# Strassen's scheme for the input projection of heads 1 to 3

## The reference: what is computed

```
xn = rmsnorm(x, norm_gain)
proj = jnp.einsum('btd,dp->btp', xn, w_in)
gb, gc, hc, zc, q, k, v, o, zm, ig, fg = jnp.split(proj, ...)
yc, conv_new = short_conv(gc * hc, conv_buf, conv_w)
y_conv = gb * yc * jax.nn.silu(zc)
...
```

## Time and profile before

| | |
|---|---|
| median of 3 runs | 1104.28 us (1104.0 to 1104.38) |
| span of the profiled execution | 1100.9 us; 3.4 us of the median lie outside it |
| TensorE busy | 1061.1 us (96%) |
| DVE, ACT, POOL busy | 540.9, 340.7, 257.9 us |
| moved by DMA | 108.74 MB, 99 GB/s in the mean |

### The profile page before, as it was taken

How to read it: one execution, slowest core, us unless ns; L and a number is a source line. 1 busy time by engine, 2 the same in 40 slices (tenths; PEclk the granted TensorE clock), 3 DMA queues, 4 the chain that set the end, 5 groups by cost and what they waited for, 6 DMA issues and landing times. The chain is left out here.

```text
span 1100.9 us, 17978 instructions
## 1 busy us (share of the span) xinstructions
PE 1061.1 (96%) x7180; PEld 602.0 (55%) x7180; DVE 540.9 (49%) x1008; ACT 340.7 (31%) x672; POOL 257.9 (23%) x333
## 2 busy tenths in 40 slices
PE   3999999999999999999999999999999999999995
PEld 3655546565666555656665556566655555444442
DVE  5786664556553434575534345655332323434333
ACT  6636434243402232434022324340213131111111
POOL 5012313021211323212113232121111121542422
PEclk9999999999999999999999999999999999999998
DMA  9484532033200322342003224310212062365651
GB/s 243 135 182 78 132 86 49 24 107 101 89 22 17 96 63 77 93 110 89 21 17 96 64 77 120 102 32 22 93 43 86 25 220 91 108 223 205 233 201 77
DMA packets 124184, 108.74 MB, mean 99 GB/s; under 512 B 42384, under 2 KB 109092, under 8 KB 124100
## 3 DMA queue, kind: packets, MB, share of 16 engines
q1 hardware_dynamic: 88192, 68.83, 22.0%
q0 software_dynamic: 7600, 25.03, 6.2%
q10 hardware_dynamic: 28308, 13.73, 4.8%
HBM read 65.43 MB, written 33.41 MB: 90 GB/s over the span
## 5 line engine op out<-in xcount | busy, mean ns | idle before, releaser
L800 PE MATMUL bank<-xTh,Wh 128*128 128x512 f16 (+2 forms) x1304 | 421.2, 342 | 5.7 <-DVE Wl L163 5.7
L801 PE MATMUL bank<-xTl,Wh 128*128 128x512 f16 (+2 forms) x1304 | 423.9, 342 | 0.0
L802 PE MATMUL bank<-xTh,Wl 128*128 128x512 f16 (+2 forms) x1304 | 423.6, 342 | 0.0
L802 PEld LDWEIGHTS bank<-xTh,Wl 128*128 128x128 f16 x1304 | 129.2, 99 | 120.3 <-issue 0.7
L800 PEld LDWEIGHTS bank<-xTh,Wh 128*128 128x128 f16 x1304 | 129.2, 99 | 113.4 <-DVE Wl L163 6.0
L801 PEld LDWEIGHTS bank<-xTl,Wh 128*128 128x128 f16 x1304 | 129.3, 99 | 108.8 <-issue 2.4
L809 PE MATMUL bank<-Wh,xTh 128*128 128x128 f16 x544 | 92.8, 219 | 0.6 <-DVE ysum L163 0.6
L811 PE MATMUL bank<-Wh,xTl 128*128 128x128 f16 x544 | 92.8, 219 | 0.0
L810 PE MATMUL bank<-Wl,xTh 128*128 128x128 f16 x544 | 92.8, 219 | 0.0
L163 ACT ACTIVATE tz<-bank 128x512 f32<-128x512 f32 x32 | 19.1, 598 | 148.4 <-PE bank L802 147.7
L672 POOL TENSOR_TENSOR ysumst<-ysum,ysumst 128x1024 f16<-128x1024 f32 x16 | 34.1, 2130 | 105.5 <-ACT ysumst L163 105.5
(11 more groups left out here) (336 smaller groups left out, 1520.5 us busy)
## 6 DMA issues: line engine op xcount, KB each, us to landing
wst<-in_w_in ACTq DMA_DIRECT2D x23, 512.0 KB, 3.9
xs<-in_x_prompt SPq DMA_DIRECT2D x22, 512.0 KB, 4.3
y_ops<-ysumst POOLq DMA_DIRECT2D x16, 512.0 KB, 3.2
w_ops<-xs SPq DMA_DIRECT2D x16, 448.0 KB, 4.5
wst<-in_w_in SPq DMA_DIRECT2D x13, 512.0 KB, 5.5
out<-xs POOLq DMA_DIRECT2D x11, 512.0 KB, 2.9
Wh<-y_ops SPq DMA_DIRECT2D x12, 448.0 KB, 3.6
Wl<-y_ops SPq DMA_DIRECT2D x12, 448.0 KB, 4.4
```

Source lines behind the costliest of these rows:

```text
L800: mm(out, wh[:, k, :], xh, start=(k == 0), stop=False)
L801: mm(out, wh[:, k, :], xl, start=False, stop=False)
L802: last = mm(out, wl[:, k, :], xh, start=False, stop=(k == KT - 1))
```

## The change

In heads 1 to 3 the eight tiles beside V are taken in four pairs, (K,Q), (GC,HC), (GB,ZC) and (O,ZM). For a pair, the two tiles of weights (each cut in two halves of the 1024) and the block of x (cut in two halves of 256 tokens and two of the 1024) are 2 x 2 matrices of parts. Seven products of 12 matmuls with 256 columns take the place of eight. Some of the products use sums of parts: three banks, XB, YB and QB, hold the results, and two of these are seeded with results formed before. ACT copies XB to YB after M1 (`y_seed`, needed by M6) and takes QB after M5 (`fifth`, tile p5s); DVE forms QB from p5s and YB after M6 (`q_seed`, needed by M7 and M3) and takes YB after M7 (`c22_read`, needed by M4). The order of the products is M1, M5, M6, M2, M7, M3, M4. The matmuls of the recurrence stand in between (`after_second`, `after_third`; a state chunk is a `stream_chunk`). The mixed tokens go by pairs too, with 24 + 36 matmuls of 80 columns, behind the pair or, for pairs 1 and 2, behind pair 1.

The parts of x and their sums (4.2 MB per block) are formed and written to DRAM in head 0: the sums by POOL (`token_sums`: one operation of 1024 and four of 256 for each of 16 units, within blocks 1 to 3), split by ACT and DVE (`S_TAKE` says behind which tile). SP streams them back in each block of heads 1 to 3.

For each head, DVE applies 9 gains to raw weights, POOL forms four sums of 512 columns per pair (`weight_sums`), and ACT and DVE split 17 tiles (`split_high`, `split_low`; `op_low` counts them, up to number 16). Part of it is done in block 3 of the head before (`prep`), the rest in block 0 (`late`). Many semaphores are merged, and some buffers and the places of w_out's operands are others.

The core of the diff:

```
+PAIRS = [(K, Q), (GC, HC), (GB, ZC), (O, ZM)]
+M1, M5, M6, M2, M7, M3, M4 = range(1, 8)
+A_11, A_12, A_21, A_22, X_S2, X_S3, X_S4, X_S1 = range(8)
...
+S_TAKE = [{}, {Q: 0, HC: 1, GB: 2, ZC: 3, O: 4, ZM: 5}, {Q: 6, HC: 7, GB: 8, ZC: 9, O: 10, ZM: 11}, {V: 12, HC: 13, O: 14, ZM: 15}]
+SPLITS = 17
+FIRST_SPLIT = [0, 5, 9, 13]
+V_SPLIT = 2
+T_SPLIT = [3, 7, 11, 15]
...
+            def load_operands(B):
+                b, at = B % NB, MIX + 4 * HALF * (B % 2)
+                sp.wait_ge(xa_out[b // 2], 16 * 8)
+                if B < NB:
+                    for i in range(2):
+                        sp.wait_ge(s_out[i], 32 * 2 * (b + 1))
+                for first, last in ((A_11, A_21), (A_22, X_S1 + 1)):
+                    for part in range(2):
+                        sp.dma_start(xT[part][:, first:last, at:at + 4 * HALF], x_ops[b, :, part, first:last, :]).then_inc(xo_in[B % 2], 16)
...
+            def weight_sums(g, p):
+                first, second = (raw_of(t) for t in PAIRS[p])
+                lo, hi = slice(0, KT // 2), slice(KT // 2, KT)
+                pool.wait_ge(op_low, splits(g, FIRST_SPLIT[p] + 1))
+                n = 16 * (g - 1) + 4 * p
+                for i, (out, x, y, op) in enumerate((
+                        (first[:, lo, :], second[:, lo, :], first[:, lo, :], ALU.subtract),
+                        (second[:, lo, :], second[:, hi, :], second[:, lo, :], ALU.subtract),
+                        (second[:, hi, :], first[:, lo, :], second[:, hi, :], ALU.subtract),
+                        (first[:, hi, :], first[:, hi, :], second[:, hi, :], ALU.add))):
+                    pool.tensor_tensor(out, x, y, op).then_inc(op_sums, 1)
+                    pool.wait_ge(op_sums, n + i + 1)
...
+                    pool.wait_ge(s_low, u - 1)
+                x, y = (t[:, :, tok0(b):tok0(b) + BT].rearrange("p (h k) t -> p h k t", h=2)[:, :, k, :] for t in (xTh, xTl))
+                pool.tensor_tensor(f, x, y, ALU.add).then_inc(s_sums, 1)
+                pool.wait_ge(s_sums, 5 * u + 1)
+                for i, (out, x, y, op) in enumerate((
+                        (f[:, 1, two], f[:, 0, two], f[:, 1, two], ALU.add),
+                        (f[:, 0, two], f[:, 0, one], f[:, 0, two], ALU.subtract),
+                        (f[:, 0, one], f[:, 0, one], f[:, 1, two], ALU.subtract),
+                        (f[:, 1, one], f[:, 1, one], f[:, 0, one], ALU.add))):
+                    pool.tensor_tensor(out, x, y, op).then_inc(s_sums, 1)
+                    pool.wait_ge(s_sums, 5 * u + 2 + i)
...
+            def pool_stream_block(g, b):
+                before = (g, b - 1) if b else (g - 1, NB - 1)
+                pool.wait_ge(t0_free, s_t0(nth(g, b), "hT") + 1)
+                y_operands(*before)
+                store_y(*before, 1)
+                if b == 0:
+                    weight_sums(g, 2)
+                store_sums(*before)
+                if b == 0:
+                    pool.wait_ge(mx_ms, g + 1)
+                    pool.tensor_tensor(hm[:, 4:5], hm[:, 3:4], halves[0:MIX, 0:1], ALU.pow).then_inc(mx_rs, 1)
+                    weight_sums(g, 3)
+                    store_mixed(g, 0)
...
+            def quarter(out, g, b, p, x_op, w_of, first):
+                wh, wl = (w_of(part) for part in range(2))
+                for k in range(KT // 2):
+                    xh, xl = (x_quarter(part, blk(g, b), x_op, k) for part in range(2))
+                    mm(out, wh[:, k, :], xh, start=(first and k == 0), stop=False, skip_group_check=not first)
+                    mm(out, wh[:, k, :], xl, start=False, stop=False, skip_group_check=not first)
+                    last = mm(out, wl[:, k, :], xh, start=False, stop=(k == KT // 2 - 1), skip_group_check=not first)
+                last.then_inc(prod, 1)
...
+            def pair(g, b, p):
+                m, (f1, f2) = pair_no(g, b, p), PAIRS[p]
+                lo, hi = slice(0, KT // 2), slice(KT // 2, KT)
+                if b == 0:
+                    pe.wait_ge(op_low, splits(g, FIRST_SPLIT[p]))
+                if m == 0:
+                    pe.wait_ge(p_free[0], NT * NB // 2)
+                    pe.wait_ge(t0_free, T0_HEAD)
+                else:
+                    pe.wait_ge(x_free, m)
+                quarter(XB, g, b, p, A_11, lambda part: W[part][:, f1, lo, :], True)
+                if m:
+                    pe.wait_ge(q_free, q_uses(g, b, p))
+                if b == 0:
+                    pe.wait_ge(op_low, splits(g, T_SPLIT[p]))
+                quarter(QB, g, b, p, X_S1, lambda part: T14[p][part][:, lo, :], True)
+                if b == 0:
+                    pe.wait_ge(op_low, splits(g, T_SPLIT[p] + 1))
+                pe.wait_ge(y_seed, m + 1)
+                quarter(YB, g, b, p, X_S2, lambda part: W[part][:, f2, hi, :], False)
+                quarter(XB, g, b, p, A_12, lambda part: W[part][:, f1, hi, :], False)
+                after_second(g, b, p)
+                pe.wait_ge(q_seed, m + 1)
+                quarter(YB, g, b, p, X_S3, lambda part: W[part][:, f2, lo, :], False)
+                quarter(QB, g, b, p, X_S4, lambda part: B22[p][part], False)
+                after_third(g, b, p)
+                pe.wait_ge(c22_read, m + 1)
+                quarter(YB, g, b, p, A_22, lambda part: T14[p][part][:, hi, :], False)
...
+            def mixed_second(out, p):
+                for k in range(KT):
+                    if k < KT // 2:
+                        parts = [[w[:, PAIRS[p][0], k, :] for w in W], [w[:, k, :] for w in T14[p]]]
+                    else:
+                        parts = [[w[:, k - KT // 2, :] for w in B22[p]]]
+                    xh, xl = xTh[:, k, 0:MIX], xTl[:, k, 0:MIX]
+                    for i, (wh, wl) in enumerate(parts):
+                        mm(out, wh, xh, start=(k == 0 and i == 0), stop=False)
+                        mm(out, wh, xl, start=False, stop=False)
+                        last = mm(out, wl, xh, start=False, stop=(k == KT - 1))
+                return last
+            def mixed_pair(out, p):
+                f1 = PAIRS[p][0]
+                split_product(out[:, 0:MIX], Wh[:, f1, :, :], Wl[:, f1, :, :], 0, KT, 0, MIX)
+                return mixed_second(out[:, MIX:2 * MIX], p)
...
+            def stream_block(g, b):
+                        mm(o, qm[:, i * MIX:(i + 1) * MIX], cs[:, i, :], start=False, stop=(i == DB - 1))
+                    mm(T1[:, 2 * P:2 * P + DV1], kwm[0:META, :], v1m[0:META, :], start=True, stop=True).then_inc(t1_full, 1)
+                pair(g, b, 2)
+                if b == 0:
+                    pe.wait_ge(op_low, splits(g, T_SPLIT[3] + 1))
+                    use_t1(s_t1(g, "oz"))
+                    mixed_pair(T1, 3).then_inc(t1_full, 1)
+                pair(g, b, 3)
...
+            def split_high(g, i):
+                src, (high, _) = split_operand(i)
...
+                mark(fn(high, src, ACT.Copy, scale=WS).then_inc(op_high, 1), op_high, splits(g, i))
+            def seed(g, b, p):
+                m = pair_no(g, b, p)
+                act.wait_ge(prod, product_at(g, b, p, M1))
+                if m:
+                    act.wait_ge(y_free, m)
+                else:
+                    act.wait_ge(p_free[1], NT * NB // 2)
+                mark(fn(YB, XB, ACT.Copy).then_inc(y_seed, 1), y_seed, m + 1)
+            def fifth(g, b, p):
+                m = pair_no(g, b, p)
+                act.wait_ge(prod, product_at(g, b, p, M5))
+                if m:
+                    act.wait_ge(c22_read, m)
+                else:
+                    act.wait_ge(xa_out[1], 16 * 8)
+                    act.wait_ge(s_sums, 5 * S_UNITS)
+                mark(fn(p5s, QB, ACT.Copy, scale=1.0 / WS).then_inc(p5_ready, 1), p5_ready, m + 1)
...
+            def gain_raw(g, t):
+                dve.wait_ge(raw_in[RAW_SLOT[t]], raw_loads(g, t))
+                w, i = raw_of(t), 9 * (g - 1) + RAW_ORDER.index(t) + 1
+                mark(tt(w, w, wide(gain, P), ALU.mult).then_inc(raw_gained, 1), raw_gained, i)
+            def split_low(g, i):
+                src, (high, low) = split_operand(i)
+                dve.wait_ge(op_high, splits(g, i))
+                mark(stt(low, src, WS, high, ALU.mult, ALU.subtract).then_inc(op_low, 1), op_low, splits(g, i))
+            def seed(g, b, p):
+                m = pair_no(g, b, p)
+                dve.wait_ge(p5_ready, m + 1)
+                dve.wait_ge(prod, product_at(g, b, p, M6))
+                mark(stt(QB, p5s, WS, YB, ALU.mult, ALU.add).then_inc(q_seed, 1), q_seed, m + 1)
+            def second_of_second(g, b, p, out, scaled):
+                m = pair_no(g, b, p)
+                dve.wait_ge(prod, product_at(g, b, p, M7))
+                ins = stt(out, YB, 1 / WS, p5s, ALU.mult, ALU.add) if scaled else stt(out, p5s, WS, YB, ALU.mult, ALU.add)
+                mark(ins.then_inc(c22_read, 1), c22_read, m + 1)
```

1180 lines of the change are left out of this document (953 added, 227 removed).

## The result

The changed kernel takes 1252.8 us (median of 4 runs, 1250.74 to 1257.65) against 1104.14: a ratio of 1.1348, 95% interval 1.1323 to 1.1374. The forecast was 1114, the range ended at 1136. The sign was right, the size was not.

What follows compares the result with a forecast made beforehand. TensorE, 96% busy, was taken to bound the kernel. 1104.3 - 52.5 of matmul time + 55.5 of waits + 7 for the clock gave 1114 us, range 1068 to 1136.

Steps and rivals of the forecast that it cites:

- Matmul time removed: Heads 1 to 3: 256-column matmuls at 0.109 us, 4.8 us gained per block; net -52.5 us with the mixed tokens.
- Seeds at nothing: Plain blocks: ACT's copies and DVE's seeds are covered by other products and cost nothing; uncovered, 0.7 us each.
- Streams at nothing: Streams from DRAM, 4.2 MB per block of about 47 us (90 GB/s), were costed at nothing.
- Point 1: Mixed pair 3 of block (g,0), three times: TensorE waits 5.6 us for split 16, 16.8 us in all.
- Point 2: Start of block (g,0): gains, factors and splits stand ahead of the seed and copy; 3.0 us each, 9.0 in all.
- Point 3: V of block (g,0): M5 of pair 1 waits for V's bank, 2.0 us each, 6.0 in all.
- Points 4 and 5: Slab split ahead of V's copy in (1,2), (2,2): 6.0 us; K's gain ahead of M7 in (1,3), (2,3): 5.6 us.
- Point 6: Head 0, blocks 1 to 3: POOL's sums of x delay scales, DVE and ACT; 10 us, from 4 to 14.
- The clock: TensorE at its lower clock level behind four waits near 5 us or over, 1.7 us each: 7 us.
- The clock rival: Clock falls in each of fourteen holes, 1.7 us each: 1131 us, or 1137 with longer POOL sums; chance 0.12.
- sum of waits: All TensorE waits from new work in heads 0 to 3 add up to 55.5 us.
- half the holes are hidden: Rival: other engines catch up during holes, so waits are 28 us and the clock 3: 1083 us; chance 0.34.

Runs made afterwards that it cites:

- e8: Changed kernel with the orders of e5 and e6 together, slabs of w_out in other places, last token unit behind the first seeds of (1,0): 1176.3 us.
- e2: Changed kernel with SP's loads of the first x stream ahead of five raw weights of head 1, the second behind ACT's last token-sum stores: 1249.1 us.
- e6: Changed kernel, heads 1 to 3 reordered: splits and gains of blocks (g,0) moved, next head's weight preparation later, partly into the next block: 1218.9 us.
- e1: Changed kernel with POOL's token sums of head 0, units 0 to 11, shrunk to 2 columns in the same place and number: 1228.2 us.
- e5: On top of e2, POOL's token sums of head 0 spread between the stores and the scales: 1235.6 us.
- e9: e8 with the tiny sums of e1 (units 0 to 11 on 2 columns): 1162.5 us.
- e7: Kernel before the change, with TensorE made to wait for POOL's idle writes ahead of tile GB in nine blocks, each another length: 1157.6 us.

## Why the prediction was wrong

Step by step, in the order of the prediction.

- *Matmul time removed.* Right: 0.109 us a step, 4.6 to 4.8 us in each block of head 3 and 4.0 to 4.8 in the slab blocks of e8, against 4.8.
- *Seeds at nothing.* Right in every block without weight work.
- *Streams at nothing, "4.2 MB per block ... 90 GB/s".* Wrong in place, right in the mean. The first streams are issued while the raw weights of head 1 and ACT's stores of token sums are under way; ACT waited the 13.04 us shown in e2 for one of these stores. The mean rate did not tell of this one 256 KB transfer issued behind several MB. e2 took the wait away; by itself that was worth 3.7 us, since POOL's sums were next.
- *Point 1, mixed pair 3.* Right: 6.31, 6.33, 6.22, in sum 18.9 against 16.8; the chain through POOL, ACT and DVE was followed from end to end.
- *Point 2, start of (g,0).* 12.29, 4.79, 5.31: 22.4 against 9.0. The last two are the chain that was worked out, some 2 us longer; of the first, 8.13 us are ACT's wait for the transfer of a token sum, which e2 made 2.71.
- *Point 3, V.* 4.87, 4.63, 4.63: 14.1 against 6.0.
- *Points 4 and 5, slab and preparation blocks.* The slab blocks lost 22.8 us and were to gain 13.2; the preparation blocks lost 28.7 and were to lose 2.0. I put one split ahead of V's copy, and one gain ahead of M7. In fact each slab brings three splits on ACT, three on DVE and four sums on POOL, each ahead of something that TensorE needs, and two slabs shared a block. ACT's timeline in the blocks (1,1) and (1,2) of the changed kernel, standing for POOL's sums and for the slab's own transfer:

```profile
457.09 1.06 ACT L203 ACTIVATE fgain<-wst 128x1024 f16<-128x1024 f32 x1 [7.26 <-POOL wst L887]
...
500.93 1.08 ACT L203 ACTIVATE fgain<-wst 128x256 f16<-128x256 f32 x2 [10.75 <-DMA wst<-in_w_out]
```

  For the slabs it was the place (that of their loads too) and not the amount, and e8 shows it: its block (3,2) has the instructions that (1,2) had in the changed kernel (50 on DVE, 45 on ACT, 17 on POOL, two slabs' work) and takes 47.4 us in place of 59.1. The -17.6 of e8's slab row is not all of this kind, since half of the slabs left these four blocks for head 3. For the preparation, e6 alone brought the two intervals from 137.1 to 115.3 us and e8 to 111.4 (108.4 before); two gains and two splits went on into the next block with it, so there place and amount are not parted.
- *Point 6, head 0: "I take 10".* The largest miss: 61.7 against 13.0 in the three intervals. The step said that DVE and ACT wait in their order "about 5 in block 1, 1 in each of the next two" and took POOL's and DVE's durations as they stand alone. Its 3.7 us ahead of the gates' matmuls came out as a hole of 5.31. The waits for cn did not: 14.94 in block 1 by the chain above, 7.11 in block 2, 9.75 in block 3; the 12.29 behind them is the first of point 2. The causes that runs show overlap and do not add up: POOL's sums in their place and their effect on DVE's durations (e1, 23 us in (0,1) and (0,2)); their place alone (e5, 13.5 us); the transfer (e2, 3.7 us). What is left in e9, 25.1 us, was not taken away; that the 14.8 in (0,3) come from head 1's preparation is argued from DVE's row, not shown, and the 10.3 in (0,1) and (0,2) have no cause named here.
- *The clock: 7.* About 48. Only four holes were to be near 5 us; there are 20 of 3.3 or more. Per hole the 1.7 us was near (1.8 to 2.75), and e7's 1.80 us hole at the full clock agrees with the earlier trace rows. The clock rival took a length "between the two that the rows show", but there is none: the hole at 42 us, behind which the clock fell, is 1.39 us long in the timeline, and that at 72.5, behind which it did not, 1.76. The rule of the Trainium skill (TensorE: Matmul & The Clock Gate, "HAM oscillation — how this bites in real kernels"), which the prediction weighed, did speak for this rival; its direction was right, and e7 bears it out in the holes of 3.38 us and more. The rival's own figure, 1131 to 1137, failed with the number of holes.

The step that failed is thus the sum of waits, 55.5 us, and in it point 6 above all: the holes measured are 147.2 us more than before. The common fault is that the six points were each worked out alone from durations measured in a kernel in which DVE was 49% and POOL 23% busy. The added busy time is 163 us on DVE (27 of it the slowing of e1) and 173 on POOL, and much of it stands ahead of something TensorE needs. What stood in the prediction as an upper bound (14 for head 0, 4 for a block) bounded the one chain that it followed. The rival *half the holes are hidden* was the wrong way round.

**Open.** No order that was tried beats the kernel before; e8 is the best at 1176.3. There the intervals of the blocks (g,0) are still 11.9 to 16.7 us longer than before, 2.2 of it by the shift; their two largest holes (ahead of ACT's ehm and DVE's cn) come to 10.5, 5.5 and 5.5, the rest is not allotted. Whether a further order hides them, or whether ACT and DVE have more work there than fits, was not tried. Neither was a kernel without preparation work in (0,3).

## What to carry to other kernels

If an engine is 96% busy, what a change adds elsewhere is free only where nothing that this engine needs stands behind it in the other engines' rows: list for each added operation the next instruction behind it that releases the bound engine, and do that for every block kind, not for one. Add about 2 us for the clock to a hole of 3.4 us or more (1.8 to 2.75 in e7), and do not count on shorter ones being free: three of 1.91 to 2.90 us were not. Of DVE and POOL running side by side, take neither's duration from where it ran alone.

## What the runs showed of the hardware

- *POOL slows DVE, not only the other way.* Beside POOL's sums a DVE scan takes 2517 ns (mean of two) in place of 1272 and a sum of two tiles 2225 in place of 684; an operation with a source in PSUM takes 693 in place of 692 (e1). DVE's busy time differs by 26.6 us for the same instructions. The Trainium skill (SBUF — State Buffer, "Who interferes with whom") says that a DVE instruction with two SBUF inputs contends with a POOL instruction that reads SBUF, and that one with at most one SBUF input outside certain modes does not; the rows agree. The prediction had weighed only POOL's side of it.
- *A hole can cost more than itself.* In e7 0.1 to 0.2 us beyond itself up to 2.70 us, 1.8 to 2.75 from 3.38 on. The length alone does not tell: the clock fell behind a hole of 1.91 us in the changed kernel and not behind one of 3.26 in e8.
- *One store behind many loads.* Stores of 256 KB landed in 2.6 us in the median in e2; in the changed kernel one held ACT for 13.04 us while the queues moved 339 GB/s.
